# One written order of steps for the first tiles of a hybrid decoder layer, and six buffers instead of four for its cached values

## The chip, the cores and the metric

One Trainium2 chip, all 8 cores, one launch. Each core computes one of the 8 prompts (2048 tokens) and 16 of the 128 sample tokens; the cores share nothing but the chip. The metric is device time in microseconds (us) of the slowest core. The engines are TensorE (PE in the profile), VectorE (DVE), ScalarE (ACT), GpSimd (POOL) and the queue SyncE (SP), which here only issues transfers.

## What is computed

The reference, cut to one layer:

```python
u = rmsnorm(x, norm_g)
proj = u @ w_in                                   # 1024 -> 8704 columns
lx, lg, sb, scg, sh, sg, q, qg, mg = jnp.split(proj, SPLIT_POINTS, axis=-1)
# A: conv(4) -> RG-LRU recurrence, gated by silu(lg), @ lru_wo
# B: silu(sg) * sb * conv3(scg * sh), @ sconv_wo
# C: 4-head attention of q into 256 memory tokens, gated by silu(qg), @ xa_wo
s = jnp.einsum('bthd,bmhd->bhtm', qh, mem_k)
p = jax.nn.softmax(s * (1.0 / math.sqrt(XA_HEAD_DIM)), axis=-1)
o = jnp.einsum('bhtm,bmhd->bthd', p, mem_v)
y = (g_a * z_a + g_b * z_b + g_c * z_c) @ w_out   # g = sigmoid(mg)
return x + y
```

For the prompt, keys and values of the 256 memory tokens are computed from mem_prompt. For the sample tokens they come from the caches cache_mem_k and cache_mem_v, 256 tokens x 512 numbers for each of the core's 16 sample tokens. The softmax and the sum over memory tokens don't depend on the order in which those tokens are laid out, as long as keys and values have the same one.

## The kernel before

**The stages.** (1) The start: 16 tiles of 128 prompt tokens, one of 16 sample tokens (tile 16) and two of memory tokens (17, 18) are loaded as float32, normalised, transposed into uT (bf16) and, as soon as tiles are there, multiplied with the first four pieces of w_in. (2) Six rounds over n, one for each 128 channels of the branches. (3) The merge: eight rounds over j (order 1, 5, 0, 2, 3, 4, 6, 7), each with two halves h of the tokens and three branches xi, in `merge_x`: a product with the gate weights, a product with the branch's output weights, tanh on ScalarE, a multiply on VectorE, additions on GpSimd. (4) The output projection with w_out, residual and final norm.

**Queues and order.** Every engine runs its own list strictly in order. `Sched` appends an instruction to its engine's list at the place where the Python code calls it, and adds the semaphore waits that its reads and writes need. So the order in which the Python steps stand is the order on all engines. Transfers are issued by SP, by POOL (all that turn float32 into bf16: weights `wl`, cached values `cv`; at the start also tiles 1 to 8 of x), and wait in the issuing engine's list.

**The start.** `START` is a list of steps. The letter says what, the number which tile: q (`n_sq`: sum of squares and root on ScalarE, lines 436 and 439), c (`n_scale`: reciprocal and scaling on VectorE, lines 447 and 449), t (`n_tr`: 8 transposes on TensorE into a half of PSUM tile PQ, line 459, and then the copy into uT with the norm weights, on VectorE, line 467), a (`awake`: products of ones that only keep TensorE busy, line 544), u (`start_unit`). A unit (s, i0, cnt) multiplies piece s (0 is q0, 1 sb01, 2 sb23, 3 sb45) with cnt tiles from tile i0 on: 16 products of 128 x 256 for two tiles, of 128 x 512 for four, and then the copy out of PSUM, on VectorE for sb23 (line 534) and on ScalarE for the others (lines 528 and 531). A t step also issues the load of tile ti + 9. PSUM has three tiles PP for units and PQ for transposes, even tiles in one half, odd ones in the other.

**The sample tokens' attention** runs in small portions between the merges (`gen_sample`, called once after most `merge_x`). Sixteen portions of keys: VectorE multiplies 256 x 512 keys with the query (line 1053) and sums (line 1057); two key buffers, loaded by SP. Then softmax. Then eight portions of values, two sample tokens b each: 16 products of 128 x 1 (tile PQ in line 374), which read the value buffers. Value buffers: four of 2 KB per partition, which lie where the two key buffers are, so their first loads wait for the last keys. After the products of b, `v_load(b + 4)` is issued on POOL. I write v6 for the values of sample token 6.

Of the kernel before, what the change touches and what calls it, by code (L numbers as in the profile page):

```python
# [10 lines left out]
BF16 = mybir.dt.bfloat16  # L11
# [6 lines left out]
TS = 16  # L18
# [38 lines left out]
NSLOT = 4  # L57
# [158 lines left out]
def build_program():  # L216
# [11 lines left out]
    ck = din("ck", [TS, NM, XW])  # L228
# [22 lines left out]
    with es:  # L251
# [65 lines left out]
        for k in ["pe", "act", "dve", "pool", "sp"]:  # L317
# [4 lines left out]
                      + [f"v{i}" for i in range(4)] + [f"ws{i}" for i in range(NSLOT)] + [f"fl{i}" for i in range(NXR)]  # L322
# [7 lines left out]
        def next_pp():  # L330
            i = state["pp"] % 3
            state["pp"] += 1
            return PP[i], tPP[i]
# [51 lines left out]
        def u_toks(lo, hi):  # L385
            if lo >= T:
                return [t_uTi[16]]
            return t_uTi[lo // 128: hi // 128]
# [65 lines left out]
        def n_tr(ti):  # L454
            src, nr, kind, c0 = tiles[ti]
            xn_, txn = xnb[ti % 4], t_xn[ti % 4]
            bankb, tbank = (PXb, tPX) if ti % 2 == 0 else (PSb, tPS)
            for kc in range(KC):
                S.op("pe", lambda e, xn_=xn_, nr=nr, kc=kc, bankb=bankb: e.transpose(bankb[:, kc * 128: kc * 128 + nr],  # L459
                                                                                    xn_[0:nr, kc * 128:(kc + 1) * 128],  # L460
                                                                                    identb[0:nr, 0:nr]),
                     reads=[txn, t_identb], writes=[tbank], inc=(kc == KC - 1))
            pview = bankb.rearrange("p (k t) -> p k t", k=KC)[:, :, 0:nr]
            dst = (uT if kind == "u" else mnT)[:, :, c0:c0 + nr]
            gcols = pT[:, 0:8] if kind == "u" else pT[:, 8:16]
            tdst = t_uTi[ti] if kind == "u" else t_mnT
            S.op("dve", lambda e, dst=dst, pview=pview, gcols=gcols, nr=nr: e.tensor_tensor(  # L467
                out=dst, in0=pview, in1=gcols.unsqueeze(2).to_broadcast([128, KC, nr]), op=ALU.mult),
                reads=[tbank, t_pT], writes=[tdst])
# [47 lines left out]

        def start_unit(name, i0, cnt_):
            views, wtk = w_get(name)
            pp, tk = next_pp()  # L520
            c0, c1 = i0 * 128, (i0 + cnt_) * 128
            for b in range(2):
                pairs = [(views[b][k], uT[:, k, c0:c1]) for k in range(KC)]
                mm_group(pp[:, b * 512:b * 512 + c1 - c0], pairs, [wtk] + u_toks(c0, c1), tk, last_inc=(b == 1))
            src = pp[:].rearrange("p (a t) -> p a t", a=2)[:, :, 0:c1 - c0]
# [16 lines left out]
        def awake(cnt):  # L542
# [5 lines left out]
        START = [  # L548
# [5 lines left out]
        rest = [(3, 0), (3, 4), (0, 8), (1, 8), (2, 8), (3, 8), (0, 12), (1, 12), (2, 12), (3, 12)]  # L554
        for ti in range(10, NT):
            START.append(("t", ti))
            if ti + 1 < NT:
                START.append(("c", ti + 1))
            START.append(("u",) + rest[ti - 10] + (4,))
            if ti + 2 < NT:  # L560
                START.append(("q", ti + 2))
        START += [("u",) + r_ + (4,) for r_ in rest[NT - 10:]]
        for what, ti, *u_ in START:
            if what == "q":
                n_sq(ti)
            elif what == "c":
                n_scale(ti)
            elif what == "a":
                awake(ti)
            elif what == "u":  # L570
                start_unit(SU[ti], *u_)
            else:
# [7 lines left out]
                if ti == 17:  # L580
# [449 lines left out]
        Vb = [carve(O_WO + i * 2048, 1024, BF16).rearrange("p (c f) -> p c f", c=2) for i in range(4)]  # L1030
# [7 lines left out]
        t_Vb = [Tok(f"Vb{i}", over=[t_Kb[i // 2]]) for i in range(4)]  # L1038

        def k_load(b):  # L1040
            S.dma("sp", f"k{b % 2}", Kb[b % 2], ck[b].rearrange("(c m) f -> m c f", c=2), writes=[t_Kb[b % 2]])

        def v_load(b):
            S.dma("pool", f"v{b % 4}", Vb[b % 4], cv[b].rearrange("(c m) f -> m c f", c=2), writes=[t_Vb[b % 4]])
# [4 lines left out]
        def gen_sample():  # L1049
            for b in range(TS):  # L1050
# [9 lines left out]
                if b + 2 < TS:  # L1060
                    k_load(b + 2)
                else:
                    v_load(2 * (b % 2))
                    v_load(2 * (b % 2) + 1)
# [21 lines left out]
            for b in range(TS):  # L1086
                vb_, tvb = Vb[b % 4], t_Vb[b % 4]
# [4 lines left out]
                if b + 4 < TS:  # L1092
                    v_load(b + 4)
# [306 lines left out]
```

How the kernel before makes its waits and increments, by code:

```python
        def run(eng, waits=waits, fn=fn, inc=inc):  # L134
            for k, v in waits:
                eng.wait_ge(sems[k], v)
            ins = fn(eng)
            if inc:
                ins.then_inc(sem, 1)
# [15 lines left out]
        def run(eng, waits=waits):  # L155
            for k, v in waits:
                eng.wait_ge(sems[k], v)
            eng.dma_start(out=out, in_=in_, **kw).then_inc(sems[semkey], 16)
# [8 lines left out]
    def wait_dma(self, keys, semkey):  # L167
        v = self.dma_cnt[semkey]
        sems = self.sems
        for k in keys:
            st = self.streams[k]
            if v and st.seen.get(semkey, 0) < v:
                st.seen[semkey] = v
                st.ops.append(lambda eng, v=v: eng.wait_ge(sems[semkey], v))
# [20 lines left out]
            def run(eng, waits=waits):  # L195
                for kk, v in waits:
                    eng.wait_ge(sems[kk], v)
```

## Time and profile before

| | |
|---|---|
| median of 3 runs | 753.0 us (lowest 751.02) |
| the profiled execution, its own time | 751.77 us |
| span of its slowest core (core 0) | 750.0 us |
| spans of the eight cores | 746.6 to 750.0 us |
| PE busy | 718.4 us, 96% |
| DVE / ACT / POOL busy | 59% / 45% / 18% |
| chain that ended last | PE 86%, DVE 4%, DMA 3%, issue 3%, ACT 2% |
| PE waiting for VectorE's scaled tiles (L449), core 0 | 10.0 us |
| PE waiting for cached values, core 0 | 3.7 us |

The span runs from the first to the last instruction of a core; the execution's own time is 1.77 us longer than the longest of them. "Busy" of an engine is the share of the span in which one of its instructions was at work. PEclk is the clock that TensorE was granted, as a share of 2.4 GHz; 0.5 is 1.2 GHz. A time in a row is counted from the span's start.

### The profile page before, as it was taken

Reading aid. Unit: us, or ns where it says so; the run is one execution under the profiler, and the core shown is the slowest. Engines: PE = TensorE matmul, PEld = TensorE weight load, DVE = VectorE, ACT = ScalarE, POOL = GpSimd, SP = SyncE. Lnnn points to the kernel's source line nnn. Section 1 sums busy time; section 2 is a strip of 40 time slices with the busy share of each in tenths; the row PEclk is TensorE's granted clock in tenths of the full one; section 3 lists DMA queues with packets and bytes.
Section 4 is the critical chain, followed back from the end, with each engine's and each line's share of the span. In section 5 each row is a group of like instructions: output and inputs, shape, how many; then the busy total and the mean of one; then the engine's idle time right before and its main releaser. Section 6 shows DMA issues by size and latency. Waiting matters only on the chain.

```text
span 750.0 us, 11337 instructions; the slowest of 8 cores (746.6 to 750.0 us)
## 1 busy us (share of the span) xinstructions
PE 718.4 (96%) x4210; PEld 354.6 (47%) x4284; DVE 443.0 (59%) x460; ACT 337.5 (45%) x431; POOL 136.8 (18%) x123
## 2 busy tenths in 40 slices
PE   5989999999999999999999999999999899999994
PEld 5754544444444444444444444444445354444442
DVE  3565332795976959869589366666623132325775
ACT  4545356768767777685772331111121112113333
POOL 4000100001010011000103233243435332322000
PEclk9999999999999999999999999999999899999998
DMA  8975260213103131030305018667756746467333
GB/s 193 267 220 100 34 144 9 50 28 57 29 2 57 29 57 29 0 57 1 71 0 127 15 26 157 153 147 159 144 82 88 115 79 112 86 190 276 156 136 148
DMA packets 28869, 71.84 MB, mean 96 GB/s; under 512 B 2464, under 2 KB 8880, under 8 KB 28688
## 3 DMA queue, kind: packets, MB, share of 16 engines
q0 software_dynamic: 12592, 36.05, 28.5%
q1 hardware_dynamic: 16080, 35.00, 14.9%
q8 instruction: 35, 0.57, 0.3%
q14 instruction: 18, 0.15, 0.1%
q10 hardware_dynamic: 144, 0.07, 0.0%
HBM read 93.27 MB, written 9.83 MB: 137 GB/s over the span
## 4 chain that ended last, share of the span: by engine, by line
PE 86%; DVE 4%; DMA 3%; issue 3%; ACT 2%; POOL 0%; DVEq 0%; ACTq 0%; POOLq 0%
PE PP L374 81%; PE PQ L374 4%; DMA R<-cv 2%; DMA R<-xp 1%; PE PQ L459 1%; ACT gA L436 1%; DVE R L793 1%; DVE gA L449 0%; DVE R L1005 0%; DVE R L1150 0%; DVE R L1154 0%; DVE R L800 0%; DVE R L994 0%; DVE R L689 0%; DVE og L690 0%
## 5 line engine op out<-in xcount | busy, mean ns | idle before, releaser
L374 PE MATMUL PP<-uT,R 128*128 128x512 bf16 (+2 forms) x2319 | 489.2, 363 | 4.5 <-DVE uT L467 1.1
L374 PEld LDWEIGHTS PP<-uT,R 128*128 128x128 bf16 x2368 | 223.8, 98 | 246.6 <-issue 6.7
L1145 ACT ACTIVATE R<-PP 128x1024 f32<-128x1024 f32 x48 | 49.2, 1025 | 204.5 <-PE PP L374 202.6
L1154 DVE SCALAR_TENSOR_TENSOR R<-R,PP 128x1024 f32<-128x1024 f32 x32 | 39.1, 1221 | 105.2 <-PE PP L374 101.0
L374 PE MATMUL PP<-R 128*128 128x512 bf16 (+1 forms) x347 | 81.1, 379 | 1.0 <-issue 0.3
L1158 POOL TENSOR_TENSOR R<-R 128x1024 f32<-128x1024 f32 x16 | 42.6, 2666 | 109.9 <-DVE R L1154 100.5
L374 PEld LDWEIGHTS PP<-R 128*128 128x128 bf16 (+1 forms) x360 | 34.2, 97 | 41.1 <-issue 0.9
L1161 POOL TENSOR_TENSOR R<-R 128x1024 bf16<-128x1024 f32 x16 | 39.9, 2496 | 48.7 <-DVE R L1154 38.8
L706 DVE SCALAR_TENSOR_TENSOR R<-R,pT 128x1024 f32<-128x1024 f32 x36 | 45.7, 1282 | 2.5
L374 PE MATMUL PP<-gB,R 128*128 128x512 bf16 x189 | 43.9, 379 | 0.2
L374 PE MATMUL PP<-gA,R 128*128 128x512 bf16 x186 | 43.6, 379 | 0.3
L1150 DVE SCALAR_TENSOR_TENSOR R<-R,PP 128x1024 f32<-128x1024 f32 x16 | 19.5, 1219 | 37.2 <-PE PP L374 20.7
L158 POOL DMA_DIRECT2D R<-wl x40 | 21.6, 542 | 88.1 <-PE PQ L374 53.9
L793 DVE SCALAR_TENSOR_TENSOR R<-R,pT 128x1024 f32<-128x1024 f32 x24 | 30.8, 1284 | 2.6
L374 PE MATMUL PP<-og,R 128*128 128x512 bf16 x125 | 30.1, 379 | 0.2
L374 PEld LDWEIGHTS PP<-gA,R 128*128 128x128 bf16 x192 | 18.8, 98 | 22.7
L374 PEld LDWEIGHTS PP<-gB,R 128*128 128x128 bf16 x192 | 18.8, 98 | 22.7
L762 DVE TENSOR_TENSOR_SCAN R<-R 128x1024 f32<-128x1024 f32 x12 | 27.9, 2321 | 1.6 <-DVE R L758 0.5
L740 DVE TENSOR_SCALAR R<-R 128x1024 f32<-128x1024 f32 x12 | 8.3, 690 | 29.4 <-ACT R L734 29.4
L467 DVE TENSOR_TENSOR uT<-PQ,pT 128x1024 bf16<-128x1024 bf16 (+1 forms) x17 | 19.7, 1167 | 8.5 <-PE PQ L459 8.3
L374 PE MATMUL PQ<-R 128*128 128x1 bf16 (+1 forms) x184 | 21.1, 229 | 3.7 <-DMA R<-cv 3.7
L768 POOL COPY SO<-R 128x1 f32<-128x1 f32 x6 | 7.1, 1184 | 93.7 <-DVE R L762 93.7
(170 smaller groups left out, 707.6 us busy)
## 6 DMA issues: line engine op xcount, KB each, us to landing
R<-wl POOLq DMA_DIRECT2D x32, 512.0 KB, 9.1
R<-ck SPq DMA_DIRECT2D x16, 512.0 KB, 5.9
y_p<-R SPq DMA_DIRECT2D x15, 512.0 KB, 2.7
R<-wl POOLq DMA_DIRECT2D x8, 768.0 KB, 10.1
uT<-xp SPq DMA_DIRECT2D x9, 512.0 KB, 7.9
R<-xp SPq DMA_DIRECT2D x8, 512.0 KB, 9.2
R<-xp POOLq DMA_DIRECT2D x8, 512.0 KB, 16.9
R<-cv POOLq DMA_DIRECT2D x16, 256.0 KB, 7.7
```

Source lines behind the costliest of these rows:

```text
L158: eng.dma_start(out=out, in_=in_, **kw).then_inc(sems[semkey], 16)
L374: S.op("pe", lambda e, l=l, r=r, i=i: e.matmul(out_ap, l, r, start=(i == 0), stop=(i == n - 1)), reads=reads, writes=[wtok], inc=(last_inc ...
L467: S.op("dve", lambda e, dst=dst, pview=pview, gcols=gcols, nr=nr: e.tensor_tensor(out=dst, in0=pview, in1=gcols.unsqueeze(2).to_broadcast( ...
L706: S.op("dve", lambda e, k=k: e.scalar_tensor_tensor(out=xc[:, lo:lo + HALF], in0=lxp[:, lo + k:lo + k + HALF], scalar=pT[:, 16 + k * 6 + n ...
L740: S.op("dve", lambda e: e.tensor_scalar(out=a2b[:, sl], in0=a2b[:, sl], scalar1=1.0, scalar2=-1.0, op0=ALU.min, op1=ALU.mult), reads=[t_a2 ...
L762: S.op("dve", lambda e: e.tensor_tensor_scan(out=a2b[:, sl], data0=thr[:, sl], data1=thi[:, sl], initial=init, op0=ALU.mult, op1=ALU.add), ...
L793: S.op("dve", lambda e, k=k: e.scalar_tensor_tensor(out=cy, in0=cinp[:, lo + k:lo + k + HALF], scalar=pT[:, 64 + k * 6 + n:65 + k * 6 + n] ...
L1145: S.op("act", lambda e, pp=pp, th_=th_: e.activation(out=th_, in_=pp[:], func=AF.Tanh, scale=0.5), reads=[tk], writes=[tth])
L1150: S.op("dve", lambda e, th_=th_, zp=zp: e.scalar_tensor_tensor(out=acc, in0=th_, scalar=1.0, in1=zp, op0=ALU.add, op1=ALU.mult), reads=[tt ...
L1154: S.op("dve", lambda e, th_=th_, zp=zp: e.scalar_tensor_tensor(out=th_, in0=th_, scalar=1.0, in1=zp, op0=ALU.add, op1=ALU.mult), reads=[tt ...
L1158: S.op("pool", lambda e, th_=th_: e.tensor_tensor(out=acc, in0=acc, in1=th_, op=ALU.add), reads=[tth, tacc_], writes=[tacc_])
L1161: S.op("pool", lambda e, th_=th_: e.tensor_tensor(out=mT[:, j, lo:hi], in0=acc, in1=th_, op=ALU.add), reads=[tth, tacc_], writes=[t_mT[j][h]])
```

## The change

1. The copies that end a transpose (step e, `n_copy`) and a unit (step k, `start_copy`) become steps of their own, and all steps stand in one written list, so that the place of each instruction on ScalarE and VectorE no longer follows from TensorE's order. u3 is done in 2-tile units for tiles 0 to 7; the fillers are 40 + 24 + 12 + 6 (before 40 + 10 + 10 + 16). The sample tokens' query product moves from step t17 to step t18.
2. Six value buffers. Two new ones lie behind the key buffers and are loaded during the keys' portions (after b = 6 and b = 8); the four old ones are now v2 to v5.
3. Keys and values are read as "(m c) f" where it was "(c m) f": each partition gets two memory tokens that are neighbours in HBM, 4 KB in one run, where it got two runs of 2 KB.

```diff
-                      + [f"v{i}" for i in range(4)] + ...
+                      + [f"v{i}" for i in range(6)] + ...
...
+        def n_copy(ti):
+            src, nr, kind, c0 = tiles[ti]
+            bankb, tbank = (PXb, tPX) if ti % 2 == 0 else (PSb, tPS)
             pview = bankb.rearrange("p (k t) -> p k t", k=KC)[:, :, 0:nr]
...
+        def start_copy(name, i0, cnt_):
+            pp, tk = su_pp[name, i0]
+            c0, c1 = i0 * 128, (i0 + cnt_) * 128
             src = pp[:].rearrange("p (a t) -> p a t", a=2)[:, :, 0:c1 - c0]
...
-        START = [
-            ("q", 0), ("q", 1), ("a", 40), ("c", 0), ("c", 1), ("t", 0), ("a", 10), ("t", 1), ("a", 10), ("q", 2), ("u", 0, 0, 2),
...
+        START = (
+            "q0 a40 c0 t0 a24 q1 e0 c1 t1 a12 e1 u0.0.2 q2 c2 q3 t2 a6 k0.0.2 c3 e2 t3 u1.0.2 e3 q4 u0.2.2 k1.0.2 "
+            "c4 u1.2.2 q5 t4 k0.2.2 c5 k1.2.2 e4 t5 u2.0.2 e5 q6 u2.2.2 k2.0.2 c6 q7 u0.4.2 k2.2.2 c7 t6 k0.4.2 "
...
-                if ti == 17:
+                if ti == 18:
...
-        Vb = [carve(O_WO + i * 2048, 1024, BF16).rearrange("p (c f) -> p c f", c=2) for i in range(4)]
+        NVB = 6
+        Vb = [carve(O_WO + o, 1024, BF16).rearrange("p (c f) -> p c f", c=2) for o in (11008, 13056, 0, 2048, 4096, 6144)]
...
-        t_Vb = [Tok(f"Vb{i}", over=[t_Kb[i // 2]]) for i in range(4)]
+        t_Vb = [Tok(f"Vb{i}", over=([t_Kb[i // 2 - 1]] if i > 1 else dead)) for i in range(NVB)]
...
-            S.dma("sp", f"k{b % 2}", Kb[b % 2], ck[b].rearrange("(c m) f -> m c f", c=2), writes=[t_Kb[b % 2]])
+            S.dma("sp", f"k{b % 2}", Kb[b % 2], ck[b].rearrange("(m c) f -> m c f", c=2), writes=[t_Kb[b % 2]])
...
-            S.dma("pool", f"v{b % 4}", Vb[b % 4], cv[b].rearrange("(c m) f -> m c f", c=2), writes=[t_Vb[b % 4]])
+            S.dma("pool", f"v{b % NVB}", Vb[b % NVB], cv[b].rearrange("(m c) f -> m c f", c=2), writes=[t_Vb[b % NVB]])
...
-                    v_load(2 * (b % 2))
-                    v_load(2 * (b % 2) + 1)
+                    v_load(2 * (b % 2) + 2)
+                    v_load(2 * (b % 2) + 3)
+                if b in (6, 8):
+                    v_load((b - 6) // 2)
...
-                if b + 4 < TS:
-                    v_load(b + 4)
+                if b + NVB < TS:
+                    v_load(b + NVB)
```

ScalarE, from its third sum of squares on (tile 2), before. CAST is the copy out of a unit's PSUM tile, PP0 of u0.0.2, PP1 of u1.0.2, PP2 of u0.2.2:

```order
7 L436 ACTIVATE gA,stat<-R 128x1024
8 L439 ACTIVATE stat<-stat,epst 128x1
9 L528 CAST R<-PP0 128x2x256
10 L436 ACTIVATE gA,stat<-R 128x1024
11 L439 ACTIVATE stat<-stat,epst 128x1
12 L531 CAST gB<-PP1 128x2x256
13 L436 ACTIVATE gA,stat<-R 128x1024
14 L439 ACTIVATE stat<-stat,epst 128x1
```

The same place in the changed kernel:

```order
7 L436 ACTIVATE gA,stat<-R 128x1024
8 L439 ACTIVATE stat<-stat,epst 128x1
9 L436 ACTIVATE gA,stat<-R 128x1024
10 L439 ACTIVATE stat<-stat,epst 128x1
11 L539 CAST R<-PP0 128x2x256
12 L436 ACTIVATE gA,stat<-R 128x1024
13 L439 ACTIVATE stat<-stat,epst 128x1
14 L542 CAST gB<-PP1 128x2x256
```

The squares of tile 3 now stand ahead of the copy of u0.0.2, and those of tile 4 ahead of the copy of u1.0.2.

VectorE at its first tiles, before (L467 is the copy of a transposed tile into uT):

```order
6 L447 RECIPROCAL stat<-stat 128x1
7 L449 TENSOR_SCALAR gA<-R,stat 128x1024
8 L447 RECIPROCAL stat<-stat 128x1
9 L449 TENSOR_SCALAR gA<-R,stat 128x1024
10 L467 TENSOR_TENSOR uT<-PQ,pT 128x8x128 x2
```

VectorE at the same place, in the changed kernel (L471 is that copy):

```order
6 L447 RECIPROCAL stat<-stat 128x1
7 L449 TENSOR_SCALAR gA<-R,stat 128x1024
8 L471 TENSOR_TENSOR uT<-PQ,pT 128x8x128
9 L447 RECIPROCAL stat<-stat 128x1
10 L449 TENSOR_SCALAR gA<-R,stat 128x1024
11 L471 TENSOR_TENSOR uT<-PQ,pT 128x8x128
```

The copy of tile 0 now stands ahead of the scaling of tile 1.

GpSimd in the merge, from the load of v0 on, before (L1158 and L1161 are the additions of a merge, wl the weights of a later round j):

```order
72 L158 DMA R<-cv 128x2x512 x2
73 L1158 TENSOR_TENSOR R<-R 128x1024
74 L158 DMA R<-cv 128x2x512 x2
75 L1161 TENSOR_TENSOR R<-R 128x1024
76 L1158 TENSOR_TENSOR R<-R 128x1024
77 L1161 TENSOR_TENSOR R<-R 128x1024
78 L158 DMA R<-cv 128x2x512 x2
79 L158 DMA R<-wl 128x3072
80 L158 DMA R<-wl 128x2048
81 L158 DMA R<-cv 128x2x512 x2
```

The same stretch in the changed kernel; v0 and v1 are loaded earlier, in its rows 63 and 67:

```order
74 L158 DMA R<-cv 128x1024 x2
75 L1171 TENSOR_TENSOR R<-R 128x1024
76 L158 DMA R<-cv 128x1024 x2
77 L1174 TENSOR_TENSOR R<-R 128x1024
78 L1171 TENSOR_TENSOR R<-R 128x1024
79 L1174 TENSOR_TENSOR R<-R 128x1024
80 L158 DMA R<-cv 128x1024 x2
81 L158 DMA R<-wl 128x3072
82 L158 DMA R<-wl 128x2048
83 L158 DMA R<-cv 128x1024 x2
```

The places of the loads are the same, but they carry other values: the pair ahead of the weights (row 78, now 80) was v4 and v5 and is v6 and v7, the pair behind them (row 81, now 83) was v6 and v7 and is v8 and v9.

## Rows read from the trace of the kernel before

**Rows 1.** Waits of PE on core 0: us in total, times, longest.

```profile
PE PQ L459 <- DVE gA L449: 10.0, 6, 3.6
PE PQ L374 <- DMA R<-cv: 3.7, 2, 2.4
```

**Rows 2.** Timeline of PE on core 0, the start: start us, us, what.

```profile
9.31 1.01 PE L459 MATMUL PQ<-identb,gA 128*128 128x128 bf16 x8 [3.56 <-DVE gA L449]
...
20.02 6.55 PE L374 MATMUL PP<-uT,R 128*128 128x256 bf16 x48
...
28.36 0.61 PE L459 MATMUL PQ<-identb,gA 128*128 128x128 bf16 x8 [1.30 <-DVE gA L449]
28.81 5.62 PE L374 MATMUL PP<-uT,R 128*128 128x256 bf16 x48
...
49.21 3.40 PE L374 MATMUL PP<-uT,R 128*128 128x512 bf16 x15
```

**Rows 3.** Windows: busy PE, PEld, DVE, ACT, POOL; then PEclk, DMA share, GB/s.

```profile
27.00:50.00 23.00, 18.31 (x182) 15.40 (x182) 15.60 (x23) 10.95 (x24) 0.00 (x0) 1.00 0.90 273
50.00:97.00 47.00, 46.72 (x321) 23.82 (x324) 20.11 (x31) 20.85 (x36) 3.26 (x6) 1.00 0.48 77
```

**Rows 4.** Timeline of PE on core 0: portions of v6, v7, and of v8, v9.

```profile
585.31 0.34 PE L374 MATMUL PQ<-R 128*128 128x1 bf16 x8 [2.37 <-DMA R<-cv]
586.94 0.35 PE L374 MATMUL PQ<-R 128*128 128x1 bf16 x8 [1.29 <-DMA R<-cv]
587.15 6.18 PE L374 MATMUL PP<-uT,R 128*128 128x512 bf16 x16
...
594.90 0.54 PE L374 MATMUL PQ<-R 128*128 128x1 bf16 x16
595.30 3.61 PE L374 MATMUL PP<-uT,R 128*128 128x512 bf16 x16
```

**Rows 5.** Timeline of ACT on core 0, the start.

```profile
23.17 0.59 ACT L531 CAST gB<-PP 128x512 bf16<-128x512 f32 x1 [5.23 <-PE PP L374]
23.65 1.06 ACT L436 ACTIVATE gA<-R 128x1024 bf16<-128x1024 f32 x1
...
25.56 1.06 ACT L436 ACTIVATE gA<-R 128x1024 bf16<-128x1024 f32 x1
```

**Rows 6.** Timeline of POOL on core 0: issue of tiles 4 and 5.

```profile
5.26 1.07 POOL L158 DMA_DIRECT2D R<-xp  x2
```

**Rows 7.** Issues of tile 4 and of tile 5, us to landing.

```profile
R<-xp POOLq DMA_DIRECT2D x1, 512.0 KB, 16.5
...
R<-xp POOLq DMA_DIRECT2D x1, 512.0 KB, 17.2
```

**Rows 8.** Lines of DVE, 27 to 50 us: busy us, mean ns, then idle before.

```profile
L467 DVE TENSOR_TENSOR uT<-PQ,pT 128x1024 bf16<-128x1024 bf16 x7 | 8.5, 1220 | 2.6 <-PE PQ L459 2.6
L449 DVE TENSOR_SCALAR gA<-R,stat 128x1024 bf16<-128x1024 f32 x6 | 4.5, 753 | 0.6
L534 DVE CAST gB<-PP 128x512 bf16<-128x512 f32 x4 | 2.8, 689 | 1.1 <-PE PP L374 1.1
```

**Rows 9.** Timeline of POOL on core 0: v4 and v5, weights, v6 and v7.

```profile
567.39 1.45 POOL L158 DMA_DIRECT2D R<-cv  x2
568.84 1.10 POOL L158 DMA_DIRECT2D R<-wl  x2
570.79 1.43 POOL L158 DMA_DIRECT2D R<-cv  x2 [0.86 <-PE PQ L374]
```

**Rows 10.** Weights' issues, median to landing; the values', min, median, max.

```profile
R<-wl POOLq DMA_DIRECT2D x32, 512.0 KB, 9.1
...
DMA to landing us min/median/max: 4.3/7.7/15.3
```

**Rows 11.** Window in and behind that wait (columns as in rows 3).

```profile
585.00:590.00 5.00, 3.40 (x23) 1.53 (x24) 0.00 (x0) 0.00 (x0) 3.23 (x3) 0.56 0.90 132
```

**Rows 12.** Timeline of DVE on core 0: the keys' portion that waited.

```profile
513.42 1.88 DVE L1053 TENSOR_TENSOR R<-R 128x1024 f32<-128x1024 f32 x1 [1.82 <-DMA R<-ck]
```

More of the change, by code:

```diff
@@ L321, in build_program @@
         dsem_names = (["cst", "wab", "wkv", "out", "wo", "fg", "prm", "kv0", "kv1"] + [f"x{i}" for i in range(NXB)] + [f"k{i}" for i in range(2)] + ["qb0", "qb1", "qsd"]
-                      + [f"v{i}" for i in range(4)] + [f"ws{i}" for i in range(NSLOT)] + [f"fl{i}" for i in range(NXR)]
+                      + [f"v{i}" for i in range(6)] + [f"ws{i}" for i in range(NSLOT)] + [f"fl{i}" for i in range(NXR)]
                       + [f"yo{i}" for i in range(5)] + [f"xq{i}" for i in range(1, NXB)])
@@ L516, in build_program @@
         wab = wab_t.rearrange("p (a n d) -> p a n d", a=2, n=NCH)
+        su_pp = {}
         def start_unit(name, i0, cnt_):
@@ L520, in start_unit @@
             pp, tk = next_pp()
+            su_pp[name, i0] = (pp, tk)
             c0, c1 = i0 * 128, (i0 + cnt_) * 128
@@ L547, in build_program @@
         SU = ("q0", "sb01", "sb23", "sb45")
-        START = [
[5 rows of a table removed]
[L554 to L563, printed above, removed]
+        START = (
[7 rows of a table added]
+        for step in START.split():
+            what = step[0]
+            ti, *u_ = [int(v) for v in step[1:].split(".")]
             if what == "q":
@@ L567, in build_program @@
                 n_scale(ti)
+            elif what == "e":
+                n_copy(ti)
             elif what == "a":
@@ L571, in build_program @@
                 start_unit(SU[ti], *u_)
+            elif what == "k":
+                start_copy(SU[ti], *u_)
             else:
@@ L1086, in gen_sample @@
             for b in range(TS):
-                vb_, tvb = Vb[b % 4], t_Vb[b % 4]
+                vb_, tvb = Vb[b % NVB], t_Vb[b % NVB]
                 for h in range(4):
```

9 rows, old and new, of the table START are left out of this document.

## The prediction

> **What bounds the kernel now.** I read the page first: TensorE is busy 96% of the span and the chain that ended last lies on it for 86%, so a gain is either less work for it (the change gives none: the same products, six fillers more) or less time in which it waits or runs at the low clock. Then its waits [rows 1]: 10.0 us for tiles that VectorE has scaled, all in the start, and 3.7 us for cached values. Of the 10.0 the first 3.56 us end at 9.31 us with the first tile [rows 2] and are outside the reach of an order of steps. The windows then show where the rest is: between 27 and 50 us TensorE is busy 18.31 of 23.00 us, though at full clock (1.00, that is 2.4 GHz); from 50 to 97 us it is busy 46.72 of 47.00 [rows 3]. So the start has some 4.7 us to give back behind 27 us, and a little ahead of it. The rest of the program has one other place, the portion of v6 and v7 [rows 4]. Of the four parts of the program only these two are on the table.
>
> **The start.** Why does TensorE wait there? ScalarE ran the copy of u1.0.2 at 23.17, after waiting 5.23 us for that unit, and only then the squares of tile 4 at 23.65 [rows 5]. Tile 4 had been there since 5.26 + 16.5 = 21.8 [rows 6, 7]; the copy that nobody was waiting for held it back by 1.8 us. The squares of tile 5 began at 25.56 [rows 5] and its transposes at 28.36 [rows 2]: 2.80 us from one to the other (squares 1.06, accumulator, root, reciprocal, scaling and four handovers). I use this 2.80 as the price of a tile's way to TensorE.
>
> Now the same with the new list. ScalarE's order is q2, q3, copy of u0.0.2, q4, copy of u1.0.2, q5. The squares of tile 4 start at its landing, 21.9, and from them to the next squares, with one copy between, it is 25.56 - 23.65 = 1.9 us [rows 5]. So q5 starts at 23.8; tile 5 has landed by then (5.78, the second of the pair, + 17.2 = 23.0) [rows 6, 7]. t5 follows at 23.8 + 2.8 = 26.6, where it was 28.36. TensorE is free for it: u1.0.2 started at 20.02 because a copy of 0.5 us stood ahead of the squares of tile 3; without it 19.5. Its three units in a row took 26.46 - 20.02 = 6.4 us, the first of them partly at the low clock (three at full clock take 5.45 of the 5.62 us from 28.81) [rows 2], so it is at t4 by 25.9 and at t5 by 26.4.
>
> From 26.6 on I find no wait longer than a few tenths. Squares and scaling run ahead of the copies and the later tiles land faster than they are used. VectorE has, for each tile, 0.9 for reciprocal and scaling and 1.2 for the copy, and 0.7 for each copy of u2 [rows 8]: for the 9 tiles t5 to t13 and 4 such copies 9 x 2.1 + 4 x 0.7 = 21.7 us. TensorE has 11 units in this stretch: 11 x 1.78 + 9 x 0.45 = 23.6 us. That cover of 1.9 us is thin, but it holds, so u0.8.4 starts at 26.6 + 23.6 = 50.2.
>
> Before, the first unit of four tiles started at 49.21 [rows 2], with 3 tiles and 3 two-tile units of that work still undone: 3 x 0.45 + 3 x 1.74 = 6.6. Like for like that is 55.8 against 50.2: a gain of 5.6 us. The windows give nearly the same another way: t5 comes 28.36 - 26.6 = 1.8 earlier, and of the 4.7 us of idle time behind 27 us all but the 1.3 ahead of t5 [rows 2] is new gain, 3.4: together 5.2. I take **5.5**. The lower bound of this term is 1.8 (all that comes behind 26.6 is given back by VectorE's queue); the upper is 6.4 (the low clock of the first unit goes as well, 1.0, and t5 waits for nothing that VectorE hasn't done by 25.4).
>
> Two edits here cost nothing. The copy of tile 0 now stands ahead of the scaling of tile 1 on VectorE, which delays t1 by the 1.2 us of that copy. From t0 at 9.31 [rows 2] I count transposes 1.0, copy 1.2, scaling 1.1, transposes 1.0, copy 1.2, with their handovers 15.0 for u0.0.2 and 16.8 for its end; tiles 2 and 3 are still on their way then, and the fillers stand there for that reason: cover 2.7 us up to u1.0.2 at 19.5. The sample tokens' query product one step later still precedes everything that reads it. Behind 50 us TensorE was full before and stays full: the gain is handed on whole, since each later transfer is released by TensorE's own progress.
>
> **The values.** v6 and v7 were issued at 570.79, behind two weight transfers at 568.84 [rows 9], and took up to 15.3 us [rows 10], to 586.8. TensorE waited 2.37 and 1.29 us for them, and its clock fell: 0.56 in that window [rows 11], so that the unit behind took 6.18 us against 3.61 [rows 4]. Price of the place: 2.37 + 1.29 + 2.57 = **6.2 us**.
>
> With six buffers the pair that waits behind those weights is v8 and v9. The pair ahead of them, at 567.39 [rows 9], is now v6 and v7, needed at 585.31 - 2.37 = 582.9; the pair in that slot was v4 and v5 and was in time for a portion that came 6.6 us earlier. v8 and v9 land where v6 and v7 did, at 585.2 and 586.8, and are needed at 594.90 - 6.2 = 588.7 and 588.9 [rows 4]. That is a margin of 3.5 and 2.1 us, not much, but no wait. The later pairs are issued 12 us and more ahead of their portions and without weights between; none waited before and each is now two places earlier. So the whole 6.2 goes. Bounds: 3.7 if the clock falls there for another reason, 6.6 if the next pairs gain a little too.
>
> What page bears on the margin: the Trainium skill, "DMA: Bandwidth & Descriptors", section "Anatomy of one DMA", fits a transfer issued from GpSimd by 2.0 us plus bytes over 436 GB/s. By that rule the two weight tiles and the two value tiles, 3.67 MB of float32 read together, need an estimated 10.4 us; this case's trace has 15.3. By the page v8 and v9 would be there five us sooner, and the second rival below would have no chance at all; by the trace it has one.
>
> **Runs of 4 KB.** No row of before shows keys or values read in such runs. Bounds: the weights, with still longer runs per partition, take 9.1 us in the median for twice the bytes of a value tile, which takes 7.7 [rows 10]; so from half of it (a gain of some 3 us in landing, worth nothing where nobody waits) to no difference. VectorE did wait for keys, 1.82 us [rows 12], but TensorE went on: a later product came without a wait. The early loads of v0 and v1 fall among the keys and may add 1 to 2 us to such a wait. The merge's multiply on VectorE then comes that much later, and with three PSUM tiles TensorE can run two products, 5 us or more, ahead of it. I take 0, bounds 0 and 1.5 of loss.
>
> **The sum.** Span 750.0 - 5.5 - 6.2 = 738.3; with 1.8 around it 740.1 us, against 751.77 of the profiled execution, 1.6% less. The median of the runs lies 1.2 above the profiled execution and the lowest 0.75 below it, so I leave the sum as it is: **740.1 us**. The other cores have the same two places, so none of them takes core 0's part as the slowest by much.
>
> **Rivals.**
> 1. *VectorE becomes the bound of the start.* The thin cover above fails: the copies of transposed tiles, now apart from their transposes, queue behind the scaling of later tiles, and units wait for uT. For it: the cover is 1.9 us in 23.6, where before VectorE was busy 15.60 of 23.00 [rows 3], and each handover counts. Against it: part of VectorE's 21.7 us can be done while TensorE waits for tile 5. It leaves 1.8 to 3 us of the start's gain: 743 us.
> 2. *The wait for values moves on to v8 and v9.* If their landing is 3 us later than v6's and v7's was, because v0 and v1 or other cores' transfers got in the way, TensorE waits 1 to 2 us and the clock falls again, 2.6: 744 us.
> 3. *Slower.* One run of 4 KB that is turned into bf16 on the way takes far longer than two of 2 KB, so that every pair of values is late. It costs nothing until v8's landing is 17.7 us after its issue (15.3 now), and it makes the kernel slower than before from 588.7 + 11.7 = 600.4, that is a landing of 29.6 us. Against it: the weights do the same conversion with longer runs in 9.1 us [rows 10]. Were it so, three or four portions would wait: 765 us.
> 4. *The steps do more than I count*, t5 without a wait and the clock high from the first unit on: 738 us or a little less.
>
> **Chances.** Forecast 0.66; rival 1 0.14; rival 2 0.10; rival 3 0.03; rival 4 0.07. The range 736 to 746.5 holds the forecast and rivals 1, 2 and 4, reaching on either side as far as the median and the lowest of the runs lie from the profiled execution and a little more, and leaves out rival 3. Two per cent (737.9 us for a median of 753.0) is about what a measurement of this kernel can tell from no change; it takes rival 4, or a forecast met with a lower scatter: faster by over 2% 0.14, within 2% 0.83, slower by over 2% 0.03.
>
> **What would show it.** In the profile after: ScalarE's squares of tile 4 at 21.9 and no copy ahead of them; t5 at 26.6; the first unit of four tiles at 50.2; PE's waits for L449 down from 10.0 to about 5; no row of PE waiting for cv, and the window of v6 and v7 at clock 1.00. A start that reaches its first four-tile unit after 52.5 is rival 1, by a wait of units for uT; a wait of 1 us or more at a portion of values is rival 2 or 3, told apart by the landing of the values. The forecast would be wrong as a whole if TensorE, once full earlier, met a new wait farther on, for example for the weights of round 0 at 97 - 5.5 us.

## The result

The changed kernel takes 739.5 us in the median of 4 runs (738.93 to 739.73), against 753.0 before; the ratio to the kernel before is 0.983, 95% interval [0.981, 0.986], so 12.6 us less with 10.8 to 14.4 in the interval. The kernel before also ran at 890.49 and 793.39 us, in a slower state in which a program on all 8 cores is now and then found whatever the kernel; all ratios here and below are of runs outside that state. Measured again beside experiments on another chip: 739.2 us, 0.981 [0.980, 0.983]. The prediction said 740.1 us, range 736 to 746.5.

The profiled execution took 738.93 us, its slowest core (now core 6) 737.4 us, the others 736.3 to 737.0. The spread over the cores has shrunk from 3.4 us to 1.1. First the page of core 6, then its waits of PE (us in total, times, longest):

```profile
PE 720.0 (98%) x4322; PEld 358.4 (49%) x4322; DVE 441.5 (60%) x460; ACT 337.6 (46%) x433; POOL 133.7 (18%) x123
...
PEclk9999999999999999999999999999999999999998
...
PE 90%; DVE 4%; issue 2%; DMA 1%; ACT 1%; POOL 0%; DVEq 0%; ACTq 0%; POOLq 0%
```

```profile
PE PQ L459 <- DVE gA L449: 3.9, 2, 2.3
PE PP L555 <- DVE epst L409: 1.6, 1, 1.6
PE PP L374 <- DVE uT L471: 0.8, 1, 0.8
PE PP L374 <- DVE R L1163: 0.6, 1, 0.6
PE PQ L374 <- DVE SO L1024: 0.5, 1, 0.5
```

TensorE is busy 98% of the span. Its wait for scaled tiles is 3.9 us in two pieces, where it was 10.0 in six [rows 1], and the row of the wait for cv is gone. The start, in the timeline of PE and in windows (columns as in rows 3), answers to rows 2 and 3:

```profile
17.42 0.81 PE L459 MATMUL PQ<-identb,gA 128*128 128x128 bf16 x8 [2.33 <-DVE gA L449]
...
19.65 6.11 PE L374 MATMUL PP<-uT,R 128*128 128x256 bf16 x48
25.60 1.06 PE L459 MATMUL PQ<-identb,gA 128*128 128x128 bf16 x16
26.49 5.40 PE L374 MATMUL PP<-uT,R 128*128 128x256 bf16 x48
...
48.83 0.61 PE L459 MATMUL PQ<-identb,gA 128*128 128x128 bf16 x8
49.28 3.62 PE L374 MATMUL PP<-uT,R 128*128 128x512 bf16 x16
```

```profile
9.00:27.00 18.00, 14.83 (x148) 12.95 (x146) 9.78 (x15) 8.32 (x19) 0.13 (x1) 0.91 0.99 244
27.00:50.00 23.00, 23.00 (x241) 20.64 (x240) 19.75 (x31) 17.97 (x39) 1.07 (x2) 1.00 0.90 272
```

Tiles 4 and 5 are transposed in one go from 25.60 on (16 products), and from then TensorE never stops: 23.00 of 23.00 us between 27 and 50, where it was 18.31. The same work that would have stood at 49.21 + 6.6 = 55.8 us on core 0 of the kernel before is reached at 49.28 on core 6 here, and on core 0 at 48.52. ScalarE shows a part of the reason (timeline of ACT, the squares of tile 4, their end, and the copy of u1.0.2 behind them):

```profile
20.92 1.06 ACT L436 ACTIVATE gA<-R 128x1024 bf16<-128x1024 f32 x1 [2.87 <-DMA R<-xp]
...
22.16 0.29 ACT L439 ACTIVATE stat<-stat,epst 128x1 f32<-128x1 f32 x1
22.36 0.59 ACT L542 CAST gB<-PP 128x512 bf16<-128x512 f32 x1
22.84 1.06 ACT L436 ACTIVATE gA<-R 128x1024 bf16<-128x1024 f32 x1
```

The squares of tile 4 wait for nothing but their transfer. On core 0 of the kernel before they stood behind the copy, at 23.65 [rows 5]; now the copy stands behind them. The values' portions of the same core, in the timeline of PE and then the issues of v6 and v7, the weights, v8 and v9 in that of POOL:

```profile
576.48 0.54 PE L374 MATMUL PQ<-R 128*128 128x1 bf16 x16
576.89 3.61 PE L374 MATMUL PP<-uT,R 128*128 128x512 bf16 x16
580.34 1.89 PE L374 MATMUL PP<-og,R 128*128 128x512 bf16 x8
582.07 0.54 PE L374 MATMUL PQ<-R 128*128 128x1 bf16 x16
```

```profile
561.45 1.10 POOL L158 DMA_DIRECT2D R<-cv  x2
562.53 1.08 POOL L158 DMA_DIRECT2D R<-wl  x2
564.48 1.08 POOL L158 DMA_DIRECT2D R<-cv  x2 [0.87 <-PE PQ L374]
```

```profile
DMA to landing us min/median/max: 5.0/8.1/17.1
```

No portion waits, the unit behind that of v6 and v7 takes 3.61 us and not 6.18 [rows 4]. But the last of these rows is worth a second look: the slowest value tile took 17.1 us. Is that v9, which now stands last behind the weights? The issues can be asked one by one, by a window around each: first v1, issued at 491.52, then v9, issued at 565.02.

```profile
R<-cv POOLq DMA_DIRECT2D x1, 256.0 KB, 17.1
...
R<-cv POOLq DMA_DIRECT2D x1, 256.0 KB, 15.3
```

So the slowest is v1, one of the two early loads: it stands behind weights too, issued at 490.43, among the transfers of keys, and isn't needed before 557. v9 took 15.3 us, as v7 did before: it landed at 580.3 and was needed at 582.3, a margin of 2.0 us. On the eight cores v9 took 14.5 to 16.4 us, and the smallest margin was 0.8 us, on core 2.

### The profile page after: what moved, and what is told of

The parts are those of the page before. It is cut to its first block, busy times and chain, and to the rows that moved or that the text cites. A ratio compares the mean times of both kernels' runs of the same rounds, so it can differ in the third digit from the quotient of the medians.

```text
span 737.4 us, 11492 instructions; the slowest of 8 cores (736.3 to 737.4 us)
## 1 busy us (share of the span) xinstructions
PE 720.0 (98%) x4322; PEld 358.4 (49%) x4322; DVE 441.5 (60%) x460; ACT 337.6 (46%) x433; POOL 133.7 (18%) x123
## 2 busy tenths in 40 slices
DMA packets 24773, 71.84 MB, mean 97 GB/s; under 512 B 2464, under 2 KB 4784, under 8 KB 24592
## 4 chain that ended last, share of the span: by engine, by line
PE 90%; DVE 4%; issue 2%; DMA 1%; ACT 1%; POOL 0%; DVEq 0%; ACTq 0%; POOLq 0%
PE PP L374 84%; PE PQ L374 5%; DMA R<-xp 1%; PE PQ L459 1%; DVE R L803 1%; DVE R L1015 0%; DVE R L1163 0%; DVE R L1167 0%; DVE R L810 0%; DVE R L1004 0%; DVE R L699 0%; DVE og L700 0%; ACT uT L1279 0%; DVE R L1276 0%; DVE R L799 0%
## 5 line engine op out<-in xcount | busy, mean ns | idle before, releaser
L374 PEld LDWEIGHTS PP<-uT,R 128*128 128x128 bf16 x2400 | 226.2, 98 | 241.8 <-issue 2.7
L1158 ACT ACTIVATE R<-PP 128x1024 f32<-128x1024 f32 x48 | 49.2, 1024 | 198.0 <-PE PP L374 196.1
L374 PE MATMUL PP<-R 128*128 128x512 bf16 (+1 forms) x360 | 83.0, 379 | 0.0
L436 ACT ACTIVATE gA<-R 128x1024 bf16<-128x1024 f32 (+1 forms) x19 | 20.0, 1052 | 12.1 <-DMA R<-xp 12.1
L815 POOL COPY SO<-R 128x2 f32<-128x2 f32 x6 | 2.7, 448 | 113.9 <-DVE R L793 113.9
## 6 DMA issues: line engine op xcount, KB each, us to landing
R<-xp POOLq DMA_DIRECT2D x8, 512.0 KB, 16.1
```

The costliest lines, as they stand in the source:

```text
L374: S.op("pe", lambda e, l=l, r=r, i=i: e.matmul(out_ap, l, r, start=(i == 0), stop=(i == n - 1)), reads=reads, writes=[wtok], inc=(last_inc ...
L436: S.op("act", lambda e, xb_=xb_, nr=nr, ti=ti: e.activation(out=junk[0:nr, :], in_=xb_[0:nr, :], func=AF.Square, accum_out=stat[0:nr, ti:t ...
L1158: S.op("act", lambda e, pp=pp, th_=th_: e.activation(out=th_, in_=pp[:], func=AF.Tanh, scale=0.5), reads=[tk], writes=[tth])
```

## The experiments

All ratios are to the kernel before, run beside them on the same chip. A line of three dots in an edit marks lines left out; what is left out is the layout of the buffers and their loads that goes with the number of buffers, or the rest of a long list.

### The two halves apart

```diff
 # e1_start_only: the changed kernel, with the value buffers and runs of before
-        NVB = 6
+        NVB = 4
...
-            S.dma("sp", f"k{b % 2}", Kb[b % 2], ck[b].rearrange("(m c) f -> m c f", c=2), ...
+            S.dma("sp", f"k{b % 2}", Kb[b % 2], ck[b].rearrange("(c m) f -> m c f", c=2), ...
...
```

> The new list of steps alone; four value buffers and runs of 2 KB as before. My theory (two separate places, each with its own price): the start's gain alone, 5.5 to 7 us, so 745 to 746.5 us and a ratio of 0.991 to 0.993 to the kernel before; TensorE waits 2.5 to 4 us for v6 and v7 as before, and its clock falls there. Rival (the start's gain is caught up by a later wait, and the buffers earn all): 750 us or more, ratio over 0.996.

Measured: 745.9 us, 0.992 [0.990, 0.993], which is 6.3 us less than before. On its slowest core TensorE waits for cv as before (waits of PE):

```profile
PE PQ L459 <- DVE gA L449: 6.9, 4, 2.9
PE PQ L374 <- DMA R<-cv: 4.3, 2, 3.4
```

The second run is the reverse:

```diff
 # e2_values_only: the kernel before, with the lines on the value buffers and the runs from the changed one
+        NVB = 6
...
+                if b in (6, 8):
+                    v_load((b - 6) // 2)
...
+                if b + NVB < TS:
+                    v_load(b + NVB)
```

> Six value buffers and runs of 4 KB alone; the old list of steps. My theory: the wait for v6 and v7 and the low clock behind it go, 6.2 us, so 745.5 us and a ratio of 0.991 to 0.993; no row of TensorE waiting for cv. Rival (the wait moves on to v8 and v9): a wait of 1 to 2 us there, ratio 0.995 or more. Theory and the first run together demand that the two ratios multiply to that of the whole change, 0.983.

Measured: 745.1 us, 0.990 [0.989, 0.992], 7.2 us less. No row of a wait for cv. The product of the two ratios is 0.982, that of the whole change 0.983 and 0.981: within the intervals the two halves add up, nothing is caught up later and nothing is counted twice. The rivals of both runs fall.

The traces divide the gain too. The first value portion (v0 and v1) is a point that every run has; in the mean of the eight cores TensorE reaches it at 562.6 us before, 562.4 with the buffers alone, 556.5 with the list alone and 556.4 in the changed kernel. From there to the end of the span it is 185.4, 180.1, 185.2 and 180.3 us. So the list earns 6.2 us ahead of that point and the buffers 5.1 behind it, in the mean of the cores; on core 0 alone, from which the prediction was worked out, it is 7.1 and 6.2.

### Buffers or runs

```diff
 # e3_six_old_runs: the changed kernel
-            ... ck[b].rearrange("(m c) f -> m c f", c=2) ... cv[b].rearrange("(m c) f -> m c f", c=2)
+            ... ck[b].rearrange("(c m) f -> m c f", c=2) ... cv[b].rearrange("(c m) f -> m c f", c=2)
```

> The whole change, but keys and values are read in runs of 2 KB as before. My theory (the number of buffers does it, the runs are worth nothing): the same time as the changed kernel, 739.5 us within 1, ratio to before 0.983, no wait for cv. Rival (the longer runs bring v8 and v9 in just in time, since in the changed kernel the slowest landing of a value tile was 17.1 to 17.4 us where 17.6 was the limit): a wait of 1 to 2 us at v8 or v9 and the low clock behind it, 742 to 744 us.

Measured: 738.8 us, 0.983 [0.981, 0.985]; no wait for cv on any core. The rival took the slowest landing for that of v8 or v9; it is v1's here as well (17.9 us on the slowest core), and v9 took 16.0 us there, 14.7 to 16.1 over the cores. (The slowest core waited 1.8 us for the weights of sb01 in the start, ahead of tile 4, and its three units behind took 5.40 us, as at full clock.) The runs of 4 KB bring no time. What they do is visible all the same: a value transfer occupies GpSimd for 0.54 us instead of 0.72, and the changed kernel moves 24773 packets where this run and the kernel before move 28869.

And the other way round:

```diff
 # e4_four_new_runs: the changed kernel with four buffers; the runs of 4 KB stay
-        NVB = 6
+        NVB = 4
...
```

> The new list and runs of 4 KB, but four value buffers. My theory: as the run with the list alone, 745 to 746.5 us, with the wait for v6 and v7 at 2.5 to 4 us. Rival (the longer runs shorten the landing behind the weights by some us): the wait is halved or gone, 740 to 743 us.

Measured: 745.6 us, 0.991 [0.990, 0.993], the same as the new list alone. Its slowest core waits 5.0 us for cv. So the buffers carry the whole of the second half.

### What the buffers change

```diff
 # e7_five_buffers: the changed kernel
-        NVB = 6
+        NVB = 5
...
-                if b in (6, 8):
+                if b == 6:
```

> The changed kernel with five value buffers instead of six: v6 goes ahead of the weights, v7 behind them, needed in the same portion. My theory (what counts is which value tile stands behind the two weight tiles, and when it is needed): TensorE waits for v7, about 2 us, and its clock may fall behind it; 741.5 to 744 us. Rival (each buffer more brings its share, or the wait is gone with any fifth buffer): no wait for cv, 739.5 us.

Measured: 743.3 us, 0.989 [0.987, 0.990]. The portion of v6 and v7 on the slowest core (timeline of PE; 8 products each):

```profile
578.84 0.34 PE L374 MATMUL PQ<-R 128*128 128x1 bf16 x8
581.15 0.34 PE L374 MATMUL PQ<-R 128*128 128x1 bf16 x8 [1.97 <-DMA R<-cv]
581.35 5.25 PE L374 MATMUL PP<-uT,R 128*128 128x512 bf16 x16
...
588.17 0.54 PE L374 MATMUL PQ<-R 128*128 128x1 bf16 x16
```

v6, ahead of the weights in GpSimd's queue, is there; v7, behind them, is 1.97 us late, just as expected. From 581.15 to the next portion it is 7.0 us where the changed kernel has 5.4 from the second half of a portion, so the clock fell there too. All cores but one show the wait (1.1 to 2.9 us), but only core 0 and core 3, which waited 2.86 us, have a slow unit behind it (5.25 and 6.39 us). Core 6 waited longer than core 0 and has none:

```profile
579.22 0.34 PE L374 MATMUL PQ<-R 128*128 128x1 bf16 x8 [2.26 <-DMA R<-cv]
579.42 3.61 PE L374 MATMUL PP<-uT,R 128*128 128x512 bf16 x16
```

The spans follow: 743.1 and 742.1 us on cores 0 and 3, 736.2 on core 1, which doesn't wait, 737.1 to 739.6 on the others. Core 0 had lost time in the start as well: it waited 1.74 us for weights there, its three units behind took 7.45 us and not 5.4 to 6.1, and it reached its first value portion at 559.46, the others at 555.7 to 557.2. A fifth buffer brings part of the gain only, because it leaves one of the two tiles behind the weights.

```diff
 # e5_weights_behind: the kernel before; rounds j but the first and last
-                w_done(f"Mg{j}")
-                w_done(f"Mo{j}")
+                held.append(j)
...
 # in the next round, behind its first value portion (v6 and v7 are then issued)
+                        if held and (h, xi) == (0, 0):
+                            jh = held.pop()
+                            w_done(f"Mg{jh}")
+                            w_done(f"Mo{jh}")
```

> The kernel before with its four buffers, 2 KB runs and old list; only the two weight transfers of each round j of the merge are issued one value portion later, so behind v6 and v7 and not ahead of them. My theory (the wait is the queue behind the weights, not the number of buffers as such): the wait for v6 and v7 falls from 3.7 us to under 0.5, and the time by about the 6 us that six buffers bring, ratio 0.991 to 0.993. Rival (four buffers are too few for the pace of the portions, whatever is ahead): a wait of 1 us or more stays at some pair, ratio over 0.995. For both: v8 and v9 have the weights ahead of them and three portions' time less than with six buffers, so a small wait may appear there.

Measured: 748.8 us, 0.996 [0.994, 0.997], 3.3 us less: about half of what six buffers bring. The wait for v6 and v7 is gone, and another has come (timeline of PE, slowest core):

```profile
588.83 0.34 PE L374 MATMUL PQ<-R 128*128 128x1 bf16 x8 [0.95 <-DMA R<-cv]
589.97 0.34 PE L374 MATMUL PQ<-R 128*128 128x1 bf16 x8 [0.80 <-DMA R<-cv]
```

That is the portion of v8 and v9, which now have the weights ahead of them. My theory said a wait of under 0.5 us at v6 and v7, which came true, and 6 us in all, which did not; the wait at v8 and v9 was 1.2 to 2.7 us by core and the ratio over 0.995, which is what the rival had said. Neither stands alone. GpSimd's timeline shows the rest:

```profile
571.56 1.10 POOL L158 DMA_DIRECT2D R<-wl  x2
577.33 2.34 POOL L1158 TENSOR_TENSOR R<-R 128x1024 f32<-128x1024 f32 x1 [4.67 <-DVE R L1154]
579.63 1.47 POOL L158 DMA_DIRECT2D R<-cv  x2
```

v8 and v9 are issued at 579.63, behind an addition that had waited 4.67 us for VectorE, and needed at 588.83 - 0.95 = 587.9. So this pair has 8.3 us, where v6 and v7 in the kernel before had 582.9 - 570.8 = 12.1 and the pair behind the weights in the changed kernel has 582.07 - 564.48 = 17.6. It took 9.1 and 9.5 us. In the kernel before, v8 and v9 took 7.8 and 8.3 us from the same place in the list (issues at 580.28 and 581.00). The queue behind the weights makes the wait, and how much of it shows depends on the time that a pair has, which the number of buffers and the additions in GpSimd's list set together.

### What in the list earns the start's gain

e6_old_copies_later is the changed kernel with the old list of steps (six buffers and runs of 4 KB stay), and against that list it only moves copies on ScalarE. The first line is the old list in the new letters; this is its first stretch, and later copies are moved in the same way:

```diff
-q2 u0.0.2 k0.0.2 a16 q3 c2 c3 ... u1.0.2 k1.0.2 q4 u0.2.2 k0.2.2 q5 u1.2.2 k1.2.2 c4 c5
+q2 u0.0.2 a16 q3 k0.0.2 c2 c3 ... u1.0.2 q4 k1.0.2 u0.2.2 q5 k0.2.2 u1.2.2 k1.2.2 c4 c5
```

> The changed kernel with the old list of steps, but each unit's copy on ScalarE stands behind the next tile's squares instead of ahead of them. Theory A (the copies on ScalarE held the start back): it has most of the start's gain, total 740 to 742 us; the transposes of tile 5 come 1.5 us or more earlier than 28.4. Theory B (TensorE's order of units and transposes and the freed copies on VectorE do most of it): total 743 to 746 us. Without any of the start's gain it would be 745.5 to 746.5.

Measured: 742.3 us, 0.987 [0.985, 0.988], between the windows of theory A and theory B. Against the buffers alone (0.990) that is 0.9965, or 2.6 us of the start's 6.3, with 0.8 to 4.5 by the two intervals. The traces give nearly the same: the first value portion comes at 560.0 in the mean of the cores, 2.4 us ahead of the buffers alone. Tile 5's transposes are early, but tile 10's wait is still there (timeline of PE, slowest core):

```profile
25.81 1.28 PE L459 MATMUL PQ<-identb,gA 128*128 128x128 bf16 x16
...
46.41 0.61 PE L459 MATMUL PQ<-identb,gA 128*128 128x128 bf16 x8 [1.88 <-DVE gA L449]
47.07 3.40 PE L374 MATMUL PP<-uT,R 128*128 128x512 bf16 x15
```

On VectorE the scaling of tile 10 stands behind the copy of u2.6.2. e11_old_both_later moves this copy and four others of u2 as well:

```diff
-u2.6.2 q11 k2.6.2 c10 t10
+u2.6.2 q11 c10 k2.6.2 t10
```

> The run with the old list and ScalarE's copies behind the squares (742.3 us), and now also VectorE's copies of u2 behind the next scaling. In that run tile 10's transposes still waited 1.88 us for a scaling that stood behind the copy of u2.6.2. Theory A (the copies, on both engines, are what cost the start; TensorE's order needs no change): the wait at tile 10 falls under 0.5 us and the total to 739.5 to 741 us. Theory B (without more units between the transposes TensorE runs dry whatever the other engines do): 741.5 to 743 us, the waits only move.

Measured: 741.7 us, 0.985 [0.984, 0.987]; the changed kernel on the same chip (e12_changed_again) 739.2.

> The changed kernel as it is, beside the two others on one chip: 739.5 us, ratio to the kernel before 0.983. It is there for the comparison.

The wait at tile 10 fell from 1.88 to 0.66 us, but 0.67 stays at tile 9 and 1.28 at tile 5, and the total missed theory A's window by 0.7 us and lies in theory B's. By the times the move on VectorE alone can't be told from nothing (742.3 and 741.7, intervals overlap); in the traces the first value portion comes 1.0 us earlier in the mean of the cores, at 559.0, against 556.4 and 557.0 in the two executions of the changed kernel. So I had to give up that the places of the units' copies alone make the start. What makes the last 2.5 us is not taken apart: the new list differs from this one in TensorE's order of units, in where the copies of transposed tiles and the squares stand, and in the fillers, of which only the fillers are tested (below).

e10_copies_at_once is the counter-test: all of the new list, but each unit's copy straight behind its unit.

```diff
-u0.2.2 k1.0.2 c4 u1.2.2 q5 t4 k0.2.2 c5 k1.2.2 e4 t5 u2.0.2 e5 q6 u2.2.2 k2.0.2 c6 q7 u0.4.2 k2.2.2 c7 t6 k0.4.2
+u0.2.2 k0.2.2 c4 u1.2.2 k1.2.2 q5 t4 c5 e4 t5 u2.0.2 k2.0.2 e5 q6 u2.2.2 k2.2.2 c6 q7 u0.4.2 k0.4.2 c7 t6
```

> The changed kernel's list with each unit's copy put straight behind its unit again on ScalarE and VectorE (the copies of transposed tiles stay where the new list has them, and so does TensorE's order). Theory A (a copy in front of squares or scaling that TensorE waits for is what cost the start): most of the start's gain is lost, tile 5's transposes come at 28 us or later, total 743.5 to 746 us. Theory B (TensorE's own order, with two-tile units up to tile 7 of sb45, gives the gain): total 739.5 to 741 us.

Measured: 753.7 us, 1.002 [1.000, 1.003], 14.5 us more than the changed kernel beside it. Theory B falls, and theory A's 743.5 to 746 was far too mild: with the buffers' 7.2 us in it, the start of this kernel is 8 to 9 us worse than the old one. It is not the old order of copies on the new list: the old kernel had the squares of tile 2 ahead of the copy of u0.0.2, here they stand behind it. So the run shows what such a place can cost, and not how much of it the old kernel paid. Waits of PE, timeline of PE and of ACT on its slowest core:

```profile
PE PQ L459 <- DVE gA L449: 12.1, 6, 3.5
PE PP L374 <- DVE stat L447: 2.2, 1, 2.2
```

```profile
32.60 1.01 PE L459 MATMUL PQ<-identb,gA 128*128 128x128 bf16 x8 [2.88 <-DVE gA L449]
...
62.81 3.40 PE L374 MATMUL PP<-uT,R 128*128 128x512 bf16 x15
```

```profile
29.31 0.59 ACT L542 CAST gB<-PP 128x512 bf16<-128x512 f32 x1 [1.00 <-PE PP L374]
29.79 1.06 ACT L436 ACTIVATE gA<-R 128x1024 bf16<-128x1024 f32 x1
...
40.60 0.59 ACT L539 CAST R<-PP 128x512 bf16<-128x512 f32 x1 [6.42 <-PE PP L374]
42.97 0.59 ACT L542 CAST gB<-PP 128x512 bf16<-128x512 f32 x1 [1.78 <-PE PP L374]
43.45 1.06 ACT L436 ACTIVATE gA<-R 128x1024 bf16<-128x1024 f32 x1
```

The squares of tile 5 begin at 29.79, behind the copies of all three units ahead of it, and its transposes follow 2.8 us later. Farther on, ScalarE sits 6.42 us in front of the copy of a unit that TensorE hasn't reached, and behind that copy stand the squares that TensorE will wait for. Tile 5 comes at 32.6, the first four-tile unit at 62.8.

### The fillers

```diff
 # e9_no_fillers: the changed kernel without three steps of fillers
-q0 a40 c0 t0 a24 q1 e0 c1 t1 a12 e1 u0.0.2 q2 c2 q3 t2 a6 k0.0.2
+q0 a40 c0 t0 q1 e0 c1 t1 e1 u0.0.2 q2 c2 q3 t2 k0.0.2
```

> The changed kernel without the fillers behind the first tile (the 24, the 12 and the 6 products of ones are left out, the first 40 stay). My theory (TensorE is ahead of tile 5 by about 1 us with them, and everything up to tile 5 has slack): the first units run at the low clock, u1.0.2 to u1.2.2 take up to 8 us instead of 5.5 to 6.4, tile 5 is reached 1 to 2 us later; total 740.5 to 742 us. Rival (fillers earn nothing): 739.5 us, first four-tile unit at the same place. Rival (the clock stays low through the whole start): 748 us or more.

Measured: 739.3 us, 0.983 [0.981, 0.984]: the same as with them. The first unit does run slower (timeline of PE, slowest core):

```profile
15.08 3.57 PE L374 MATMUL PP<-uT,R 128*128 128x256 bf16 x16 [1.48 <-DVE uT L471]
...
25.86 1.06 PE L459 MATMUL PQ<-identb,gA 128*128 128x128 bf16 x16
...
49.55 2.75 PE L374 MATMUL PP<-uT,R 128*128 128x512 bf16 x12
```

u0.0.2 takes 3.57 us, twice the 1.9 of a unit at full clock, and over the window from 9 to 27 us core 0 was granted 0.81 where the changed kernel has 0.91. The three units behind took 5.4 to 5.9 us, not up to 8. Tiles 4 and 5 are transposed at 25.86, against 25.60 in the changed kernel: the squares of tile 4 begin as soon as the tile has landed, at 20.32, and nearly all that TensorE loses ahead of that is slack. The first value portion comes at 556.5 in the mean of the cores, with the fillers at 556.4. My expectation of 1 to 2 us was wrong, the rival that fillers earn nothing here was right.

## Why the prediction came out as it did

**The sum.** 740.1 us forecast, 739.5 measured. It was made of 5.5 us for the start and 6.2 for the values; alone they measured 6.3 [5.0 to 7.7] and 7.2 [5.7 to 8.6]. The forecast was a sum for core 0, and there the traces give 7.1 us ahead of the first value portion and 6.2 behind it: the values were met, and the term that was mis-sized is the start's, by 1.6 us. Core 0's span was to be 738.3 us and is 736.7. That the time came out only 0.6 us under the forecast is in part luck: the slowest core is now core 6 (737.4), and the median of the runs lies 0.6 us above the profiled execution.

**The start.** Squares of tile 4 expected at 21.9, seen at 20.58 on core 0 and 20.92 on core 6; t5 expected at 26.6, seen at 25.3 on core 0 and about 26.0 on core 6; the first four-tile unit expected at 50.2, seen at 48.52 and 49.28. The first 1.3 of these 1.7 us on core 0 are the landing of tile 4: 20.4, where the prediction took 21.8 from the kernel before. On that execution's eight cores it had landed at 20.2 to 21.8, so the forecast rested on one of the two latest cores; it is a scatter that the steps don't make. The rest is the work between t5 and that unit, 23.6 us by the prediction, 23.2 in the trace. PE's waits for L449 were to be about 5 us: 3.9 and 4.5. The thin cover on VectorE held: it was busy 19.75 of 23.00 us and TensorE 23.00, so rival 1 did not come true. The cause that the prediction named, a copy in front of the squares, is shown by e6 for some 2.5 us of it, and e10 shows in the other direction how much such a place can cost. What the prediction did not see is that with the units' copies moved the rest of the old list still keeps some 2.5 us of waits (e11): the whole gain needs the new list together with the moved copies, and which part of the new list earns it is open.

**The values.** The price of the wait with the clock behind it, 6.2 us on core 0, is what core 0 gained; its cause, the two weight transfers ahead in GpSimd's queue, is shown by e5, where the wait at v6 and v7 goes when they are moved, and by e7, where v6 ahead of them is in time and v7 behind them is late. That the wait doesn't move on to v8 and v9 was right, and the margin was sized right too: forecast 3.5 and 2.1 us, on core 6 3.2 and 2.0, with landings of 14.4 and 15.3 us as before. On core 2 v9 had 0.8 us, so rival 2 was nearer on some cores than the forecast for core 0 said. The prediction set the 15.3 us beside an estimate of 10.4 for all four transfers; counted from the same moment as that estimate, the first weight transfer at 568.84, v7 took 18.0 us.

**Runs of 4 KB.** Nothing, as taken; the slower rival built on them had nothing in it. (The landing of v8 from which that rival would begin to cost, 17.7 us, should read 588.7 - 570.8 = 17.9.)

**Two per cent.** The step that failed is the sentence that 2% is about what a measurement of this kernel can tell from no change, and with it 0.83 on "within 2%" as if that were near to nothing. The runs showed in its place a fall of 1.7% with an interval of 0.24% on either side, and 0.15 to 0.2% in the experiments, so a gain clear of no change. No wait, cost or overlap of the sum has to be given up for that: the sum itself forecast 1.6% less, which such a measurement can tell, and the chances should have said so. Whether the gain is under 2% is closer: 0.981 [0.980, 0.983] in the second measurement touches it.

## What to carry to other kernels

With engines that work strictly in order, a copy that nobody waits for must not stand ahead of work that the bound engine waits for; give every instruction its own place in the list, and move the bound engine's order and the others' together: the new list with its copies in place was 2.5 us faster than the old one with moved copies, and the same order of TensorE was 14.5 us slower with each copy straight behind its unit. For a stream of small transfers that shares a queue with large ones, count which transfer stands behind the large ones and how long until it is needed: two buffers more took the wait away, a fifth buffer alone or a later place of the weights only a part of it. Look at the margin that is left, not only at the wait that is gone, and look up which transfer it was that took longest before you reason from it.

## What the runs showed of the hardware

- A value transfer of 512 KB of float32 into 256 KB of bf16, issued from GpSimd, took 0.54 us to issue with one run of 4 KB per partition (changed kernel) and 0.72 with two of 2 KB (e3); v9, behind the same two weight transfers, landed after 14.5 to 16.4 us and 14.7 to 16.1 over the eight cores.
- In e7 single waits of 1.97 and 2.86 us (cores 0 and 3) were followed by a unit of 5.25 and 6.39 us where 3.61 is usual, and single waits of 1.11 to 2.26 us on the five other cores that waited by none. The wait of 1.88 us in e6's start was followed by none either (3.40 us for 15 products of the next unit). In these runs the length of the wait does not settle which of the two happens.
- 42 products of ones at the start raised the granted clock from 9 to 27 us on core 0 from 0.81 to 0.91, and over the eight cores from 0.72 to 1.00 to 0.91 to 1.00, and were worth nothing in the total (739.3 and 739.5 us): behind them TensorE waited for tiles that were still landing.
